# Side work of a hybrid decoder layer moved into the bursts of its attention items

## The reference, cut to what matters

```python
def rwkv7_mix(u, ...):
    u = u + (token_shift(u) - u) * mu
    r, k, v, xw, xa, xg = split(u)
    decay = exp(-exp(-softplus(-(w0 + tanh(xw) @ w2)) - 0.5))    # z: tanh(xw) @ w2
    a = sigmoid(a0 + xa @ a2)
    g = sigmoid(xg) @ g2
    kk = heads(k * k_k); kk = kk / max(norm(kk), 1e-12)          # the K sum
    k = k * (1 + (a - 1) * k_a)
    y = rwkv7_scan(r, decay, k, v, kk, a)
    y = (y - mean(y)) * rsqrt(var(y) + GN_EPS) * lnx_g + lnx_b   # per head
    bonus = sum(r * k * r_k, per head) * v                       # the bonus sum
    return (y + bonus) * g
def fox_mix(u, ...):
    for blk in range(4):      # 128 queries each, keys up to the block's end
        scores = q[blk] @ k.T * scale + bias, causal
        out[blk] = softmax(scores) @ v
```

## Time and profile before

| | us |
|---|---|
| median of 3 runs | 2748.56 |
| lowest, highest | 2748.4, 2748.79 |
| the profiled execution | 2746.44 |
| its span, first to last instruction | 2744.5 |
| mean granted clock of TensorE | 0.998 |

### The profile page before, as it was taken

How to read it: one execution, slowest core, us unless ns; L and a number is a source line. 1 busy time by engine, 2 the same in 40 slices (tenths; PEclk the granted TensorE clock), 3 DMA queues, 4 the chain that set the end, 5 groups by cost and what they waited for, 6 DMA issues and landing times.

```text
span 2744.5 us, 41129 instructions
## 1 busy us (share of the span) xinstructions
PE 2688.0 (98%) x15562; PEld 2140.8 (78%) x15562; DVE 1168.4 (43%) x1717; ACT 1022.7 (37%) x1460; POOL 221.1 (8%) x348
## 2 busy tenths in 40 slices
PE   8999999999999999999999999999999999999998
PEld 6776776776777688888888888888888888888787
DVE  6654653663663535333333333333333333334543
ACT  5435534534644424433223332233332222234421
POOL 3001210210111103000000000000000000011300
PEclk9999999999999999999999999999999999999999
DMA  4221231231132432322233222332223322223332
GB/s 168 87 76 58 69 94 59 70 86 56 65 91 90 133 98 98 107 99 94 87 95 107 99 93 85 98 107 99 92 88 95 108 98 93 95 86 108 106 119 76
DMA packets 108136, 255.91 MB, mean 93 GB/s; under 512 B 35288, under 2 KB 37848, under 8 KB 108024
## 3 DMA queue, kind: packets, MB, share of 16 engines
q1 hardware_dynamic: 105920, 247.10, 28.3%
q0 software_dynamic: 2112, 7.34, 0.8%
HBM read 245.43 MB, written 8.98 MB: 93 GB/s over the span
## 4 chain that ended last, share of the span: by engine, by line
PE 72%; issue 18%; POOL 3%; DVE 3%; ACT 2%; DMA 1%; SPq 1%; POOLq 0%; DVEq 0%; ACTq 0%
PE bank L318 23%; PE bank L315 23%; PE bank L319 23%; PE bank L356 1%; POOL probs L1097 1%; POOL scratch_pool L129 1%; DVE w_lo L310 1%; DMA raw<-w_mix 1%; ACT w_hi L303 0%; POOL sg_t L1089 0%; SPq L1305 0%; PE bank L481 0%; POOL carried L1124 0%; POOL M_t L1111 0%; PE bank L510 0%
## 5 line engine op out<-in xcount | busy, mean ns | idle before, releaser
L310 DVE TENSOR_TENSOR w_lo<-raw,w_hi 128x1024 fp32r<-128x1024 f32 (+1 forms) x484 | 546.1, 1130 | 965.2 <-ACT w_hi L303 964.5
L303 ACT ACTIVATE w_hi<-raw 128x1024 fp32r<-128x1024 f32 (+1 forms) x484 | 471.7, 975 | 963.2 <-PE bank L319 940.4
L315 PE MATMUL bank<-hn_hi,w_hi 128*128 128x512 f32 x1664 | 648.1, 389 | 0.0
L319 PE MATMUL bank<-hn_hi,w_lo 128*128 128x512 f32 x1664 | 647.3, 389 | 0.0
L318 PE MATMUL bank<-hn_lo,w_hi 128*128 128x512 f32 x1664 | 647.3, 389 | 0.0
L315 PE MATMUL bank<-in_hi,w_hi 128*128 128x512 f32 x1088 | 455.9, 419 | 29.9 <-DVE in_lo L1689 11.6
L318 PE MATMUL bank<-in_lo,w_hi 128*128 128x512 f32 x1088 | 441.7, 406 | 0.0
L319 PE MATMUL bank<-in_hi,w_lo 128*128 128x512 f32 x1088 | 428.0, 393 | 0.0
L318 PEld LDWEIGHTS bank<-hn_lo,w_hi 128*128 128x128 f32 x1664 | 312.3, 188 | 65.5 <-issue 0.5
L315 PEld LDWEIGHTS bank<-hn_hi,w_hi 128*128 128x128 f32 x1664 | 312.3, 188 | 65.2 <-issue 0.5
L319 PEld LDWEIGHTS bank<-hn_hi,w_lo 128*128 128x128 f32 x1664 | 312.3, 188 | 64.8
(11 more groups left out here) (240 smaller groups left out, 2123.3 us busy)
## 6 DMA issues: line engine op xcount, KB each, us to landing
raw<-w_gu SPq DMA_DIRECT2D x176, 512.0 KB, 3.4
raw<-w_mix SPq DMA_DIRECT2D x116, 512.0 KB, 3.6
raw<-w_down SPq DMA_DIRECT2D x64, 384.0 KB, 3.1
raw<-w_down SPq DMA_DIRECT2D x64, 320.0 KB, 2.9
raw<-ple_gate SPq DMA_DIRECT2D x32, 512.0 KB, 3.4
raw<-w_mix SPq DMA_DIRECT2D x28, 384.0 KB, 3.2
h_t<-xT SPq DMA_DIRECT2D x4, 1024.0 KB, 6.2
out<-h_t POOLq DMA_DIRECT2D x16, 256.0 KB, 2.3
```

What stands on the lines that cost most here:

```text
L303: nc.scalar.activation(w_hi[:, ring_slots(par2, half), 0:cols[half]], raw[:, half, 0:cols[half]], ACT.Copy).then_inc(hi_ready, 1)
L310: nc.vector.tensor_tensor(w_lo[:, s, 0:cols[half]], raw[:, half, 0:cols[half]], w_hi[:, s, 0:cols[half]].bitcast(F32), ALU.subtract).then_ ...
L315: nc.tensor.matmul(out, w_h, x_hi, start=start, stop=False, skip_group_check=True)
L319: return nc.tensor.matmul(out, w_l, x_hi, start=False, stop=stop, skip_group_check=True)
```

## The change

It changes at which steps the side work of slabs 0 to 5 is issued, and its place within a burst.

- In a burst the preparation now comes first, then the group norm, then the attention item.
- Both means stand at step 2, both variances at step 5, both gates at step 10 of slab 0 (before: 1 and 2, 4 and 5, 7 and 9).
- z and a are issued together, at step 5 of slab 0 and step 7 of slab 3 (before: steps 8 and 10 of either). a's product has a bank of its own for that: b6 for tile 0, b7 for tile 1.
- The gates of tile 0 are written to b6 too, so with a following group they wait for a's sigmoid.
- The K sum stands at step 9 of slab 1 and step 6 of slab 4 (before: 5), the keys from steps 12 and 11 on (before: 9), the bonus sum at step 13 of slab 2 and step 10 of slab 5 (before: 11).

```diff
-BONUS_AT = 11
+Z_AT, K_SUM_AT, KEYS_AT, BONUS_AT = (5, 7), (9, 6), (12, 11), (13, 10)
...
+    a_bank = b6, b7
+
     def pe_rwkv_prep(pe, s, kt, g):
...
-        if kind == 0 and kt == 8:
+        if kind == 0 and kt == Z_AT[ft]:
...
                     pe.wait_ge(S("fox_v_tok_ready"), 2 * g)
+                    pe.wait_ge(S("y_centered"), 2 * g)
...
                 pe.wait_ge(S("v_st_ready"), f)
+                if not (isinstance(g, int) and g == 0):
+                    pe.wait_ge(S("o_ready"), 2 * g - 1)
...
-        if kind == 0 and kt == 10:
-            pe.wait_ge(S("sigmoid_z_ready"), f + 1)
-            nc.tensor.matmul(aux[:], w2a2[0:LORA, 1, tok(ft)], xa_t[0:LORA, :], start=True, stop=True
+            nc.tensor.matmul(a_bank[ft][:], w2a2[0:LORA, 1, tok(ft)], xa_t[0:LORA, :], start=True, stop=True
                              ).then_inc(S("a_done"), 1)
-        if kind == 1 and kt == 5:
+        if kind == 1 and kt == K_SUM_AT[ft]:
...
-    def pe_finish(pe, s, kt, gp):
+    def pe_finish(pe, s, kt, gp, last_group=False):
...
+        if kt == 10:
+            pe.wait_ge(S("g2_landed"), 16 * (gp + 1))
+            pe.wait_ge(S("sig_g_ready"), 2)
+            pe.wait_ge(S("y_centered"), 2 * gp + 2)
+            pe.wait_ge(S("y_log_ready"), 2 * gp + 1)
+            if not last_group:
+                pe.wait_ge(S("a_ready"), 2 * gp + 3)
+            for ft in range(2):
+                for k in range(2):
+                    last = nc.tensor.matmul(gate_bank[ft][:], g2_t[:, k, tok(ft)], sig_g[:, k, :], start=k == 0,
+                                            stop=k == 1)
+                last.then_inc(S("g_done"), 1)
...
                         if s < 6:
+                            yield from pe_rwkv_prep(pe, s, kt, g)
                             if gp is not None:
+                                pe_finish(pe, s, kt, gp)
                                 pe_attention(pe, s, kt, gp)
-                                pe_finish(pe, s, kt, gp)
-                            yield from pe_rwkv_prep(pe, s, kt, g)
```

More of the change, by code:

```diff
@@ L391, in pe_rwkv_prep @@
             nc.tensor.matmul(aux[:], const(C_BLK), t1[:], start=True, stop=True).then_inc(S("k_sum_done"), 1)
-        if kind == 2 and kt == BONUS_AT:
+        if kind == 2 and kt == BONUS_AT[ft]:
             if isinstance(g, int) and f == 0:
@@ L432, in layer @@
     mean_bank, var_bank, gate_bank = (b5, b6), (b7, b5), (b6, b7)
-    def pe_finish(pe, s, kt, gp):
+    def pe_finish(pe, s, kt, gp, last_group=False):
         if s != 0:
             return
-        if kt in (1, 2):
-            ft = kt - 1
+        if kt == 2:
             pe.wait_ge(S("Y_ready"), NC * gp + NC)
-            nc.tensor.matmul(mean_bank[ft][:], const(C_BLK), AR[:, ft, 1, :], start=True, stop=True
-                             ).then_inc(S("y_sum_done"), 1)
-        if kt == 2:
+            for ft in range(2):
+                nc.tensor.matmul(mean_bank[ft][:], const(C_BLK), AR[:, ft, 1, :], start=True, stop=True
+                                 ).then_inc(S("y_sum_done"), 1)
@@ L443, in pe_finish @@
             pe.wait_ge(S("fox_v_tok_ready"), 2 * gp + 1)
             pe_fox_values(pe, gp, 1)
[L445 to L461, removed]
+        if kt == 5:
+            for ft in range(2):
+                pe.wait_ge(S("y_squared"), 2 * gp + ft + 1)
+                nc.tensor.matmul(var_bank[ft][:], const(C_BLK), AR[:, ft, 0, :], start=True, stop=True
+                                 ).then_inc(S("y_var_done"), 1)
@@ L687, in act_rwkv_prep @@
             nc.scalar.activation(t1[:], t2[:], ACT.Square, scale=gp_col(K_K)).then_inc(S("k_square_ready"), 1)
-        if kind == 1 and kt == 6:
+        if kind == 1 and kt == K_SUM_AT[ft] + 1:
             act.wait_ge(S("k_sum_ready"), f + 1)
@@ L692, in act_rwkv_prep @@
             nc.scalar.activation(t1[:], t1[:], ACT.Exp, scale=-0.5, bias=cb(CB_KK)).then_inc(S("k_rnorm_ready"), 1)
-        if kind == 2 and kt == BONUS_AT - 6:
+        if kind == 2 and kt == 5:
             act.wait_ge(S("rk_ready"), f + 1)
@@ L697, in act_rwkv_prep @@
             nc.scalar.activation(bonus_high[:, ft, :], t1[:], ACT.Copy).then_inc(S("rk_high_ready"), 1)
-        if kind == 2 and kt == BONUS_AT + 1:
+        if kind == 2 and kt == BONUS_AT[ft] + 1:
             act.wait_ge(S("bonus_done"), f + 1)
@@ L737, in act_finish @@
             act_fox_values(act, 2 * gp + 1, 1)
[L738 to L741, removed]
+        if kt == 3:
+            for ft in range(2):
+                act.wait_ge(S("y_centered"), 2 * gp + ft + 1)
+                nc.scalar.activation(AR[:, ft, 0, :], AR[:, ft, 1, :], ACT.Square).then_inc(S("y_squared"), 1)
         if kt == 6:
@@ L922, in dve_rwkv_prep @@
                                            op0=ALU.mult, op1=ALU.mult).then_inc(S("key_step"), 1)
-        if kind == 1 and kt == 10:
+        if kind == 1 and kt == KEYS_AT[ft] + 1:
             dve.wait_ge(S("key_step"), 6 * f + 2)
@@ L928, in dve_rwkv_prep @@
             nc.vector.tensor_tensor(B_t[:, ft, :], t1[:], pi_t[:], ALU.mult).then_inc(S("key_step"), 1)
-        if kind == 1 and kt == 11:
+        if kind == 1 and kt == KEYS_AT[ft] + 2:
             nc.vector.tensor_scalar(a_t[:], a_t[:], -1.0, gp_col(K_A), ALU.add, ALU.mult
@@ L935, in dve_rwkv_prep @@
                                            ).then_inc(S("key_step"), 1)
-        if kind == 1 and kt == 12:
+        if kind == 1 and kt == KEYS_AT[ft] + 3:
             dve.wait_ge(S("key_step"), 6 * f + 6)
@@ L972, in dve_finish @@
             return
[L973 to L978, removed]
+        if kt == 2:
+            for ft in range(2):
+                dve.wait_ge(S("y_sum_done"), 2 * gp + ft + 1)
+                nc.vector.scalar_tensor_tensor(out=AR[:, ft, 1, :], in0=mean_bank[ft][:], scalar=-1.0 / HD,
+                                               in1=AR[:, ft, 1, :], op0=ALU.mult, op1=ALU.add
+                                               ).then_inc(S("y_centered"), 1)
         if kt in (7, 10):
@@ L989, in dve_finish @@
                                            ).then_inc(S("y_plus_bonus"), 1)
-        if kt in (8, 11):
-            ft = (kt - 8) // 3
+        if kt in (11, 12):
+            ft = kt - 11
             dve.wait_ge(S("g_done"), 2 * gp + ft + 1)
```

12 lines of the change are left out of this document (6 added, 6 removed).

## The result

The changed kernel takes **2773.26 us** (median of 4 runs, 2771.39 to 2774.88), the kernel before 2748.48 in the same session (2746.55 to 2748.79). The ratio is 1.0094, with a 95% interval of 1.0082 to 1.0106: slower, by 0.9%. The forecast was 2768.6. The sign and the place were right, the size was short: the profiled execution took 2772.99, 26.6 more than the 2746.44 of before, where the sum said 20.0. By the ratio on the 2748.56 the forecast started from, the result is 2774.4, which is 0.4 above the range's upper end of 2774.

A forecast was written before the change was run, and what follows sets the result against it. TensorE bounds the kernel, busy 98% of the span. Per group 5.2 - 0.3 + 1.7 + 1.2 - 1.4 = 6.4; three groups 19.2, group 0 +1.1, tail -0.3: +20.0, 2768.6 us median; range 2760 to 2774.

The forecast's parts named there:

- The new wait: Slab 0 of groups 1 to 3: the gates wait for a's sigmoid, 5.2 us (bounds 4.8 and 5.7).
- Pause and bursts together: Slab 0, groups 1 to 3: wait of 5.2 less 0.3 for fewer bursts and gaps, per group.
- Slabs 1 and 2: Late tile 0 keys delay the low part, so slab 2's bonus sum waits 1.2 us per group (bounds 0.5 and 2).
- slabs 3 to 5: -1.4: Slabs 3 to 5 get shorter through fewer waits and earlier keys, -1.4 us per group (bounds -2.4 and 0).
- stay within 0.2: Slab 4: the squares of K, set by ScalarE's and VectorE's chain, move by no more than 0.2 us.
- The clock term: Slab 0: the pause brings TensorE's half-rate clock, costing 1.7 us per group (ends 0 and 2.5).
- Group 0: Group without attention: bonus sums wait more, +0.7 in slab 5 and +0.4 in slab 2, +1.1 us in all.
- The tail: After the last group, no a to wait for and the first logarithm ready before step 10: -0.3 us.
- (a): Rival: merging pays, 39 bursts saving a 0.4 us tail each, -15.6 us to 2733; chance 3%.
- (b): Rival: the clock doesn't fall behind the pauses, +14.9 us, 2763.5; chance 13%.
- (c): Rival: late keys cost more than 1.2 and slabs 3 to 5 give nothing back, +6.6 us, 2775; chance 8%.
- (d): Rival: the change does not act, wait on a met early, 2746 to 2750 us; chance 2%.

The follow-up runs named there:

- sigmoids_ahead: The changed kernel with ScalarE's two sigmoids issued at the lora pair's step in slabs 0 and 3, ahead of that step's attention exponential; 2745.94 us, ratio 0.9993.
- tile0_keys_back: The changed kernel with K's norm sum, keys and bonus sum of tile 0 back at steps 5, 9 and 11; 2773.26 us, ratio 1.0096.
- scores_ahead: The changed kernel with the old order inside a burst: attention first, then the finish, then the lora pair; 2758.62 us, ratio 1.0036.
- sigmoids_slab3: The changed kernel with the sigmoids issued ahead for tile 1 alone (slab 3, step 7), slab 0 as changed; 2767.64 us, ratio 1.0073.
- fill_the_pause: The changed kernel with six extra unused 128x512 fp32 products before the wait on a's sigmoid; 2767.08 us, ratio 1.0070.
- sig_unmerged: sigmoids_ahead with tile 0's K sum, keys and bonus sum at old steps, and means, variances, gates apart (gates at 8 and 10); 2745.89 us.
- gates_other_bank: The changed kernel with tile 0's gates in bank 5 and tile 1's in bank 7, not waiting for a's sigmoid; 2759.81 us, ratio 1.0043.
- sig_all_back: sigmoids_ahead with tile 0's K sum, keys and bonus sum at old steps, tile 1's keys at 9 and bonus sum at 11; 2746.58 us.
- sig_bonus12: sigmoids_ahead with tile 0's K sum, keys and bonus sum at old steps, tile 1's keys at 10 and bonus sum at 12; 2745.33 us.

## Why the prediction was right, and where it wasn't

**The new wait** (forecast 5.2, measured 5.03) was right in place, size and releaser, because each of its parts was read from rows. They are the late scores (9.13 into the slab, forecast 9.11), 0.8, and three table loads with their work. Pause and bursts together came to 5.1 a group for a forecast of 4.9. sigmoids_ahead shows that nothing else in slab 0 is worth more than 0.5.

**Slabs 1 and 2** were right: 0.0 and +1.17 for 0 and +1.2. The profile counts 0.92 idle there, and by the starts the bonus sum is 1.08 late (527.15 + 0.23 = 527.38, and 528.46). tile0_keys_back shows tile 0's late steps as the cause.

**The step that failed is "slabs 3 to 5: -1.4"**, and in it the sentence that the squares of K "stay within 0.2". The term came out at +0.1, 0.0 and +0.9, 5.3 us more in all than forecast, and the squares at 1.4 later. I moved the scores behind the new products in slab 0 and worked out what that does to ScalarE; in slab 3 the same edit puts 1.72 us ahead of item 10's scores, and I did not carry it through, though ScalarE's order has item 10's exponential in front of z's sigmoid in both kernels. With the scores ahead of the pair again (scores_ahead) the squares are within 0.2 of before, and with the sigmoid ahead of the exponential (sigmoids_slab3) the term is -1.55. Group 3's 0.9 is the clock: it fell once behind the wait of 2.3 that stands where 0.8 was, slab 4 took 19.40 for 17.80, and slab 5 gave 0.7 of that back (15.90 for 16.64).

**The clock term was mis-sized**: 7.0 us in slab 0 for 5.1, shown by fill_the_pause. The direction was right. The third group lost 30.20 - 27.12 = 3.1, which is above the end of 2.5 that I kept, the second 2.2, the fourth 1.7. The Trainium skill (TensorE: Matmul & The Clock Gate, "HAM oscillation — how this bites in real kernels") has idle gaps send TensorE back to the half rate and the penalty paid again each time. The runs agree for the 5.0 us pauses, and the pauses of 2.3 to 2.5 were followed by a low clock only in 10 of 18 cases (below).

**Group 0** was forecast at +1.1. Its slabs 2 and 5 grew by 0.48 and 0.67, as forecast (0.4 and 0.7). But the fall at 63.5 was in the profile of before and not in that of after, -1.65 in slab 0. Of 14 profiled executions with that same pause (1.94 to 1.98), 5 show the fall; fill_the_pause has it and the change has not, with the same code up to there. So a sum made from one profile carries it as an error of 1.7. That it was missing after the change is luck, and it hid 1.7 of what the two terms above had missed. **The tail** came to +0.2 for -0.3: merged gates there too stand later than apart (23.16 against 22.29 in sig_unmerged).

**The rivals.** (a) is refuted twice, by the result and by sig_unmerged, which has slab 0 shorter with separate bursts. (b), no fall, was wrong in all three groups. (c) named 2775 and came closest in number; half of its mechanism was wrong (the late keys cost 1.17, not 2), half came true by another cause (slabs 3 to 5 gave nothing back). Its number was luck, since it had no extra loss to the clock and no missing fall in group 0. (d) was wrong.

## What to carry to other kernels

Work put ahead of a product delays whatever the other engines have behind that product, in every place where the edit applies: follow it through each engine's order, also where TensorE has nothing to lose. Here one order on ScalarE decided 27 us, while merging the bursts, the visible part of the change, gained nothing in itself. When a step moves, try the places between the old and the new as well: a step too early waits for its input and a step too late makes its reader wait. With the finish apart, tile 0's norm sum at steps 5, 6 and 7 gave 2745.89, 2744.57 and 2741.38.

## What the hardware showed that I had not expected

Filling a pause of TensorE with useless products made the kernel faster by 6.2 us (fill_the_pause), and the clock of that stretch stayed at the 2.4 GHz level.

Whether a pause of TensorE is followed by the 1.2 GHz level differs from one execution to another over a band of pause lengths. Counted over the profiles of the kernel before, the change, gates_other_bank, fill_the_pause, tile0_keys_back, scores_ahead, sigmoids_slab3, sig_all_back and sig_bonus12, in groups 1 to 3:

| TensorE idle, us | pauses | followed or cut by a low clock |
|---|---|---|
| 5.03 | 9 | 9 |
| 2.8 to 2.9 | 3 | 3 |
| 2.3 to 2.5 | 18 | 10 |
| 1.9 to 2.2 | 9 | 2 |

No pause of 1.0 to 1.8 us in these groups was followed by one; the other five kernels have only such. The loss differs too: after the same pause of 5.03 the groups of one execution lost 2.2, 3.1 and 1.7 us. In the second group the low stretch began before the pause was over (264.0, the gates at 266.3), where it costs nothing until work resumes; in the fourth it began with the work. Why one or the other happens was not tested.
